# Query tiles of a hybrid attention layer in the order 7,0,6,1,5,2,4,3, normed rows turned one by one beside the output projection, turns of a key tile ahead of the value products

## The reference, cut to what matters

```python
def one_block(i):                      # one query tile of 128 tokens, lax.map over 8
    # three branches, each a masked softmax with ALiBi, 8 heads in 2 KV groups
    o_c = softmax(q @ k_c) @ v_c       # 63 compressed keys
    # block importance from p_c picks 8 blocks of 64 keys
    o_s = softmax(q @ k_g) @ v_g       # selected blocks, keys 0..own position
    o_w = softmax(q @ k_w) @ v_w       # sliding window of 512 keys
    return gate0 * o_c + gate1 * o_s + gate2 * o_w

def layer_tail(x, o_a, o_b, lp):
    o = concat([rmsnorm(o_a), rmsnorm(o_b)])
    x = x + o @ w_out
    h = rmsnorm(x)
    return x + (silu(h @ w_gate) * (h @ w_up)) @ w_down
```

## Time and profile before

| what | value |
| --- | --- |
| median of three runs | 1849.69 us |
| profiled execution, whole | 1841.58 us |
| its span, first to last instruction | 1839.9 us |
| tensor engine (PE) busy | 1683.0 us, 91% of the span |
| VectorE (DVE) busy | 719.5 us, 39% |
| ScalarE (ACT) busy | 420.6 us, 23% |
| GpSimd (POOL) busy | 278.9 us, 15% |
| chain that ended last: PE, DVE, issue, DMA, ACT | 85%, 6%, 3%, 2%, 2% |
| feed-forward weights (512 KB), issue to landing | 3.8 to 6.1 us |

### The profile page before, as it was taken

How to read it: one execution, slowest core, us unless ns; L and a number is a source line. 1 busy time by engine, 2 the same in 40 slices (tenths; PEclk the granted TensorE clock), 3 DMA queues, 4 the chain that set the end, 5 groups by cost and what they waited for, 6 DMA issues and landing times.

```text
span 1839.9 us, 24807 instructions
## 1 busy us (share of the span) xinstructions
PE 1683.0 (91%) x9131; PEld 1267.4 (69%) x9131; DVE 719.5 (39%) x1321; ACT 420.6 (23%) x887; POOL 278.9 (15%) x296
## 2 busy tenths in 40 slices
PE   7999998698768898999997799999999999999995
PEld 4564455587356555655443398998998998998993
DVE  3220333222145666667212215335335335335337
ACT  2111112122124444445111121112112112112112
POOL 2210121211300000000001013113113113113112
PEclk9999999698968999999997899999999999999998
DMA  8220000533720000000201111211211211211202
GB/s 304 96 72 22 25 1 9 141 92 104 206 92 4 4 4 4 7 1 1 103 1 35 35 35 35 69 34 34 68 34 34 68 34 34 68 34 34 68 11 92
DMA packets 92670, 98.91 MB, mean 54 GB/s; under 512 B 6680, under 2 KB 74873, under 8 KB 92505
## 3 DMA queue, kind: packets, MB, share of 16 engines
q1 hardware_dynamic: 70122, 76.55, 13.3%
q0 software_dynamic: 4880, 12.96, 2.3%
q10 hardware_dynamic: 17600, 8.47, 1.7%
HBM read 90.81 MB, written 11.34 MB: 56 GB/s over the span
## 4 chain that ended last, share of the span: by engine, by line
PE 85%; DVE 6%; issue 3%; DMA 2%; ACT 2%; ACTq 1%; POOL 0%; POOLq 0%; SPq 0%; DVEq 0%
PE bankpair L356 13%; PE bankpair L1984 9%; PE bankpair L1986 9%; PE bankpair L1985 9%; PE bankpair L1611 6%; PE bankpair L2025 5%; PE bankpair L1673 4%; PE bankpair L2027 4%; PE bankpair L2026 4%; PE bankpair L1657 3%; PE bankpair L868 3%; PE bankpair L1572 2%; PE bankpair L1574 2%; PE bankpair L1543 1%; DMA work<-in_state_win_kv 1%
## 5 line engine op out<-in xcount | busy, mean ns | idle before, releaser
L1984 PE MATMUL bankpair<-h2T_high,w_high 128*128 128x344 f32 x1056 | 338.1, 320 | 0.0
L1985 PE MATMUL bankpair<-h2T_low,w_high 128*128 128x344 f32 x1056 | 337.4, 320 | 0.0
L1986 PE MATMUL bankpair<-h2T_high,w_low 128*128 128x344 f32 x1056 | 337.4, 320 | 0.0
L356 PE MATMUL bankpair<-work 128*128 128x512 f32 (+1 forms) x640 | 256.7, 558 | 0.8 <-DMA work<-in_w_in 0.8
L2136 DVE TENSOR_TENSOR x_all<-x_all,bankpair 128x512 f32<-128x512 f32 x352 | 224.8, 683 | 1.1
L2116 DVE TENSOR_TENSOR kT_space<-kT_space,bankpair 128x344 f32<-128x344 f32 x66 | 33.9, 513 | 450.7 <-ACT kT_space L2062 450.7
L356 PEld LDWEIGHTS bankpair<-work 128*128 128x128 f32 x640 | 120.2, 191 | 123.0 <-issue 116.1
L1984 PEld LDWEIGHTS bankpair<-h2T_high,w_high 128*128 128x128 f32 x1056 | 198.9, 188 | 0.9
L1985 PEld LDWEIGHTS bankpair<-h2T_low,w_high 128*128 128x128 f32 x1056 | 198.6, 188 | 1.0
L1986 PEld LDWEIGHTS bankpair<-h2T_high,w_low 128*128 128x128 f32 x1056 | 198.7, 188 | 0.0
L2049 POOL TENSOR_TENSOR w_low<-work,w_high 128x1024 fp32r<-128x1024 f32 x44 | 105.1, 2411 | 558.0 <-ACT w_high L2044 557.9
(11 more groups left out here) (303 smaller groups left out, 2127.9 us busy)
## 6 DMA issues: line engine op xcount, KB each, us to landing
work<-in_w_gate SPq DMA_DIRECT2D x22, 512.0 KB, 4.9
work<-in_w_up SPq DMA_DIRECT2D x22, 512.0 KB, 6.1
work<-in_w_down SPq DMA_DIRECT2D x22, 512.0 KB, 3.8
x_all<-in_x_prompt SPq DMA_DIRECT2D x16, 512.0 KB, 8.5
work<-in_w_in SPq DMA_DIRECT2D x4, 2048.0 KB, 10.0
work<-in_cache_kv_cmp SPq DMA_DIRECT2D x32, 128.0 KB, 2.8
work<-in_cache_kv_cmp POOLq DMA_DIRECT2D x32, 128.0 KB, 2.9
work<-in_cache_kv_slc POOLq DMA_DIRECT2D x32, 128.0 KB, 3.8
```

The source lines that it names most:

```text
L356: ins = pe.matmul(pb(at_n % 4)[:, 0:w], hT[:, k, P * t:P * t + P], wslot[c % 2][:, k, 0:w], start=(k == 0), stop=(k == KD - 1))
L1984: pe.matmul(out, wh, high, start=(k == 0), stop=False)
L1985: pe.matmul(out, wh, low, start=False, stop=False)
L1986: ins = pe.matmul(out, wl, high, start=False, stop=(k == KD - 1))
```

## The change

All lists of stage 4 go by `ORDER` instead of 0 to 7; `TURN` is a tile's place in it and takes the tile number's place in buffer parities and semaphore counts. In a slot T stands ahead of PV and EX. The start of a tile's window turns is moved on where the tile before isn't finished by then. In the tail each H2N is issued ahead of a WA or WO and its H2T behind it; `h2` has two buffers, and turned rows alternate between bank pairs 3 and 2. The first gate/up chunk takes the free score bank pair.

```diff
+ORDER = [7, 0, 6, 1, 5, 2, 4, 3]
+TURN = {t: n for n, t in enumerate(ORDER)}
+LAST = ORDER[-1]
...
-    h2 = at(1536, [D], regC)
+    h2 = [at(1536, [D], regC), at(512, [D], regC)]
...
+            first_w = max(first_w, done + 4 - len(key_tiles(i, "w")) - 1)
...
         events.append(("QK", slot))
         events += first_x.get(slot, [])
+        if slot in turns:
+            events.append(("T", turns[slot]))
         if slot in products:
...
         events.append(("EX", slot))
-        if slot in turns:
-            events.append(("T", turns[slot]))
...
-    events += [("H2N", NT), ("H2T", NT), ("OBQ", NT - 1), ("OBN", NT - 1), fill.pop(0), ("OBT", NT - 1)]
+    events += [("OBQ", LAST), ("OBN", LAST), ("H2N", NT), fill.pop(0), ("OBT", LAST), ("H2T", NT)]
     turned = 1
     while fill:
         e = fill.pop(0)
+        done = events.index(("WO", tail_tiles[turned])) if ("WO", tail_tiles[turned]) in events else len(events)
+        ready = any(x[0] in ("WA", "WO") for x in events[done + 1:])
+        if ready:
+            events.append(("H2N", tail_tiles[turned]))
         events.append(e)
...
+        if ready:
+            events.append(("H2T", tail_tiles[turned]))
+            turned += 1
+    events += [("H2N", LAST), ("GU", 0), ("H2T", LAST), ("GU", 1)]
...
-        return bank[3] if e in h_at else bank[s_at[e] % 2]
+        return bank[3 - h_at[e] % 2] if e in h_at else bank[s_at[e] % 2]
...
                 else:
-                    pe.wait_ge(h_taken, len(h_at))
+                    pe.wait_ge(h_taken, len(h_at) - 1)
                 gate_up_chunk(pe, 0, 0, a).then_inc(gu_ready, 1)
             elif name == "H2T":
                 pe.wait_ge(h2_ready, tail_order(a) + 1)
...
+                order = h_at[e]
+                if order == 0:
                     pe.wait_ge(o_copied, len(branches))
+                    pe.wait_ge(x_taken, len(x_at))
+                elif order == 1:
+                    for x in range(2):
+                        pe.wait_ge(pt_taken[x], len(items))
+                else:
+                    pe.wait_ge(h_taken, order - 1)
...
+        pe.wait_ge(act_ready, 1)
         gate_up_chunk(pe, 0, 0, 2).then_inc(gu_ready, 1)
```

More of the change, by code:

```diff
@@ L1352, in row_sum @@
     def row_sum(i, kind):
[L1353 removed]
+        return sums_w if kind == "w" else sums_s[TURN[i] % 2]
     def probs(kind):
         return p_win if kind == "w" else p_slc
[L1360 removed]
+    units = [(i, kind, h) for i in ORDER for kind in "ws" for h in range(NH)]
     unit_at = {u: n for n, u in enumerate(units)}
[L1362 removed]
+    branches = [(i, kind) for i in ORDER for kind in "wcs"]
     branch_at = {b: n for n, b in enumerate(branches)}
@@ L1384, in place_branch @@
         return slot + len(parts)
[L1386 to L1392, removed]
+    for turn, i in enumerate(ORDER):
+        start = SLOTS * turn
+        first_w = start + NH + 1
+        if turn:
+            last_turn = ORDER[turn - 1]
+            done = place_branch(last_turn, "s", start + 1) + 1
+            for n, name in enumerate(("OBQ", "OBN", "OBT")):
+                at_slot(first_x, done + 1 + n, name, last_turn)
+            first_w = max(first_w, done + 4 - len(key_tiles(i, "w")) - 1)
         else:
             for n, name in enumerate(("OBQ", "OBN", "OBT")):
-                at_slot(first_x, 1 + n, name, NT)
+                at_slot(first_x, start + 1 + n, name, NT)
         at_slot(last_x, start, "CS", i)
@@ L1417, in build_program @@
         events.append(("EX", slot))
-        if slot in turns:
-            events.append(("T", turns[slot]))
-    final = branch_items((NT - 1, "s"))
-    tail_tiles = [NT] + list(range(NT))
-    fill = [("WO", NT)] + [(name, t) for t in range(NT) for name in ("WA", "WO")]
+    final = branch_items((LAST, "s"))
+    tail_tiles = [NT] + ORDER
+    fill = [("WO", NT)] + [(name, t) for t in ORDER for name in ("WA", "WO")]
     events += first_x.get(len(units), []) + [fill.pop(0)]
@@ L1506, in tail_order, with load_qaug, wait_qaug @@
     def tail_order(t):
[L1508 to L1513, removed]
+        return 0 if t == NT else TURN[t] + 1
+    def load_qaug(pool, turn):
+        if turn >= 2:
+            pool.wait_ge(s_ready, s_at["QK", unit_at[ORDER[turn - 2], "s", NH - 1]] + 1)
+        pool.dma_start(qT_aug[64:KAUG, turn % 2].rearrange("p g n -> p (g n)"), C["qaug"][ORDER[turn]])\
+            .then_inc(qaug_ready[turn % 2], 16)
+    def wait_qaug(eng, i):
+        eng.wait_ge(qaug_ready[TURN[i] % 2], 16 * (TURN[i] // 2 + 1))
     def stage4_sync(sp):
@@ L1520, in stage4_sync @@
         sp.wait_ge(s_ready, s_at["QK", len(units) - 1] + 1)
-        for t in range(NT):
+        for t in ORDER:
             sp.dma_start(x_all[:, t, :], x_dram(t)).then_inc(x_in[t], 16)
@@ L1581, in stage4_tensor @@
             elif name == "SELT":
-                pe.wait_ge(sel_ready, a - 3)
+                pe.wait_ge(sel_ready, 1 + sum(t >= 4 for t in ORDER[:TURN[a]]))
                 for g in range(NG):
@@ L1683, in take_probs @@
         copy(pT[n % 2][0:r, g, :], pb(4 + g)[0:r, :]).then_inc(pt_taken[g], 1)
-    sq_before = sum(e[0] == "WO" for e in events[:events.index(("OBQ", NT - 1))])
+    sq_before = sum(e[0] == "WO" for e in events[:events.index(("OBQ", LAST))])
     def stage4_scalar(act):
@@ L1752, in stage4_pool @@
                 inv_rms(pool, chain.link, ssb[0:n, a:a + 1], rb[0:n, a:a + 1], 512).then_inc(ob_inv, 1)
-            elif name == "QT" and a[1] == 0 and a[0] >= 2:
-                load_qaug(pool, a[0])
+            elif name == "QT" and a[1] == 0 and TURN[a[0]] >= 2:
+                load_qaug(pool, TURN[a[0]])
             elif name == "WO":
@@ L1811, in add_branch @@
             dst = (ob if first else tmp).rearrange("p (g r d) -> p g r d", g=NG, r=NR)
-            if first and i:
-                wait_x(dve, ("OBT", i - 1))
+            if first and TURN[i]:
+                wait_x(dve, ("OBT", ORDER[TURN[i] - 1]))
             src = x_bank.rearrange("p (r g d) -> p g r d", r=NR, g=NG)
```

108 lines of the change are left out of this document (51 added, 57 removed).

## The result

The changed kernel takes 1796.22 us (median; 1794.12 to 1797.80) against 1848.76 (1841.35 to 1851.47) for the kernel before on the same chip: ratio 0.9721, interval 0.9691 to 0.9751. The forecast was 1804. On another chip the same kernel took 1803.84 against 1849.57 (see the last experiment). The profiled execution took 1794.12, its span is 1792.4 against 1839.9.

What follows compares the result with a forecast made beforehand. Loss was put in the tail's turns of normed rows and small losses across attention. -14 (attention), -22 (tail waits) and -9.6 (tail clock) make -45.6: 1796 by the profiled execution, 1804 as median; range 1782 to 1828.

Steps and rivals of the forecast that it cites:

- The waits of the tail: Tail: idle falls from 26.1 to 4.1, gain 22; new waits of 1.6 (sample rows' turn) and 2.5 (second gate/up chunk).
- The tail's clock: Tail: low clock costs 10.6 in turns, half products and gate/up chunk; about 1 stays, gain 9.6.
- The longest chain: Tail: add, square and readout, copy, subtractions, next norm take 6.1 us, covered by the next half product plus turns, 6.87 + 0.9.
- Rival D: Tail: norms come late by 1.7 each despite the second buffer, +12, 1816; chance 0.09, alone or with B.
- Turns before products: Attention: products no longer wait for copies of turns just made, slots become dense; bounds 19 us gain, 42 loss.
- Attention: Attention stage: time over dense work falls from 82 to 68, gain 14; stage lasts about 340, moved key tiles included.
- dense work: Attention: scores, turns and products, priced from slots where nothing waits at the high clock, sum to 264 of 346.
- VectorE sets them: Wide window halves: VectorE, busy throughout, sets 17, 19.5, 20.5 and 21 us for tiles 7, 6, 5, 4; 24 over dense.
- Rival A: Attention: thin halves run wholly at 1.2 GHz, +73, 1877, slower than before; chance 0.04.
- B: Attention gains nothing: wide window halves lose what narrow ones win, 82 over dense stays, 1818; chance 0.15.
- C: Attention gains more: time over dense work falls to 50, as dense slots keep the clock up, 1786; chance 0.16.
- the main case: Whole kernel: attention and tail gain as summed, 1791 to 1816; chance 0.54.

Runs made afterwards that it cites:

- the last experiment: The changed kernel itself, unedited, run once more on another chip: 1803.84 us, ratio 0.9758, attention 349.83.
- Experiment 7: Changed kernel with the sample rows' turn behind the next half product and step 0's second and third gate/up chunks swapped: 1792.10 us, ratio 0.9719.
- Experiment 3: Kernel before with the new tail alone; query tiles in ascending order, turns at the end of the slot: 1814.02 us, ratio 0.9826.
- experiment 5: Changed kernel with the tail's old list, turns in groups behind an output product; both norm buffers and bank pairs stay: 1835.17 us, ratio 0.9935.
- experiment 6: Changed kernel with one norm buffer and one bank pair for turned rows, the new tail list kept: 1805.75 us, ratio 0.9767.
- experiment 1: Changed kernel with query tiles in ascending order again; turns ahead of products and new tail stay: 1810.74 us, ratio 0.9799.
- experiment 4: Changed kernel with a key tile's turns behind the value product but ahead of the exp: 1808.95 us, ratio 0.9791.
- experiment 9: Changed kernel without VectorE's sums of block importance for tiles 6, 5 and 4: 1799.70 us, ratio 0.9750.
- experiment 10: Experiment 7's kernel with the previous tile's norm and turn placed behind the selection in the window halves of tiles 5 and 4: 1795.85 us, ratio 0.9730.
- experiment 8: Kernel before without the sums of block importance for tiles 5 to 7: 1845.58 us, ratio 0.9999.

## Why the prediction was right, point by point

**The waits of the tail** came out as worked out: 26.1 to 1.6 + 2.5, at the two places named, and the second wait by the steps named (ScalarE's copy 1.02, subtractions 1.29, start at 1016.38). Experiment 7 confirms both as waits that can be taken away.

**The tail's clock.** 0.90 over the whole became 0.99, and the tail is 143.98 against a forecast of 145. Experiment 3, with the same work in the tail as before, gives the term by itself: 33.5 us, against 22 + 9.6 = 31.6. The clock goes with the waits: with 27.1 of them back (experiment 5) it is 0.92, with none (experiment 7) 1.00; the one that is left ahead of the sample rows' turn takes 1.7 of clock in some executions.

**Which part of the tail's edit does it.** The prediction argued with the two buffers and bank pairs and the new places at once. Experiments 5 and 6 part them: the places give all of it, the buffers nothing beside them. The longest chain, 6.1 us by the earlier trace rows, fits beside the next half product even where each norm waits for the turn before it. Rival D (norms 1.7 late each) was not seen: line 1653 doesn't wait for a norm once in the profile after (in experiments 1 and 3, with two turns behind the last product, one waits 1.5).

**Turns before products.** Here the step was wrong in its size and in what it hangs on, although its mechanism is right: the product's second half did wait for the copy just made. The working bounded the gain by "0.29 x 66 = 19", as if each key tile won the 0.29 that a slot of 512 keys shows in the earlier trace rows. The loop is a floor of 2.88 for the slot; what is won is 2.88 less the slot's own dense sum: 0.55 at 128 keys, 0.26 at 512, 0.08 at 640 and nothing beyond. In the old order, where most turns stand in wide slots, the slots at full clock gain 4.9 in all; in the new one, which brings the turns into narrow slots, 12.3 or 9.9 (experiment 3). A second part of the gain isn't in the working. It named the waits for the exp (11.2) and for the selection (6.4) as the longest kinds, but between them stood 6.6, with another kind 7.6, in which products waited for ScalarE's copy behind the exp, and these went too (experiment 4). The prediction counted order and turns apart, and its sum for attention came out near the shorter profile, since it took the slots as dense and the order as moving cover.

**Attention.** Forecast 340, measured 341.38: 346.01 - 4.63, with 7.4 moved in, so 12 like for like against 14. By its own parts: dense work 264 (its terms add up to 263) + 7.4, so 70 over it, against 68. The wide window halves took 19.25, 20.85, 22.04 and 21.28 (tiles 7, 6, 5, 4) against 17, 19.5, 20.5 and 21, together 5.4 more than forecast, which the other halves made up. "VectorE sets them" is right for tile 6 (experiment 9); in tile 4's half it is VectorE's order and not its load (experiments 9 and 10), and tile 5's lies between. What the prediction would have VectorE show, busy throughout, isn't there: 18.32 of 20.85.

**Rival A, the clock,** wasn't seen as such: attention has 0.92 in one profile and 0.89 in the other, near the 0.90 and 0.88 of the kernel before and experiment 8, although thin halves are indeed where it falls (0.83 and 0.89 in the window halves of tiles 6 and 5). But it decides how good a single figure for attention is: 341.4 or 349.8 for one program. The forecast's third digit in attention is luck. On the second chip the median of 1803.84 stands on the forecast of 1804; the like-for-like gain in its profile is 3.6 against the profile before and 8.7 against experiment 8, whose clock is as low, and not 12.

**Rivals B and C.** C (attention's overhead down to 50) is not reached in any run: it is 70 in the profile after. In the second one it is 349.8 - 271.4 = 78, near the 82 of B. The forecast by the profile's own time was 1796, and B by the same reckoning 1810. The two profiled executions took 1794.12 and 1802.67: the first stands near the main case, the second half way to B, as the clock alone makes 8.5 of the 14 between them. Against a profile with as low a clock B is wrong too (8.7 gained in attention, experiment 3), but what is certain of the gain is the tail.

## What to carry to other kernels

Where a product uses what was turned in the same slot, look for a loop turn, copy, second half of the product, next turn: its length is a floor that hides under wide slots and bites once narrow ones get the work, so put the turn ahead of the product of an earlier tile before moving work into narrow slots, and price such an edit slot by slot against the floor. Put it ahead of the exp as well, where the engine that takes the exp also copies the turns. Where a chain of add, norm and copy fits beside one long product, issue it one product ahead and turn behind it; try the place alone before paying for a second buffer. Compare stretches that differ by a few us only after the same program has been profiled twice, or over the slots at full clock in both profiles.

## What the runs showed that was not expected

The clock's falls are not a fixed property of a program. In dense stretches executions agree to 0.01 us or so (slots of 2.33 in each; the 94 slots at full clock in both profiles of the changed kernel differ by 0.11 in all, the other 34 by 8.3), and behind a thin stretch or a short wait the same code takes one of two lengths: a slot 2.96 or 5.38 us, a tail 143.98 (three profiles) or 142.28 to 142.29 (three profiles). Nearly all of the 8.5 us between the two profiles of the changed kernel is in four halves (tile 0's window 20.42 and 22.70, tile 7's selected 25.11 and 26.18, tile 6's window 20.85 and 25.05, tile 3's window 20.05 and 22.51), less 1.6 where the first profile took longer (tile 1's window, 22.99 and 21.35).
